# Odd layer: shares of the output projection as seven products of half depth; neighbourhood attention's bias tables by GpSimd

## The reference, cut to what matters

```
bias = rpb[:, d_row[:, None, None, :, None], d_col[None, :, :, None, :]]
s_loc = jnp.einsum('brnqhd,brnjwhd->bhrnqjw', qb, k_band.astype(f32)) + bias.astype(f32)[None]
s_loc = jnp.where(col_valid[:, :, None, :], s_loc, NEG_INF)
```

## Time and profile before

| | us |
|---|---|
| median of 3 runs | 3266.69 (3261.67 to 3269.23) |
| the profiled execution, its own time | 3264.15 |
| its span | 3262.4 |
| PE busy | 3063.6 (94%) |
| DVE busy | 1571.3 (48%) |
| ACT busy | 719.9 (22%) |
| POOL busy | 9.6 |

### The profile page before, as it was taken

The page is one execution under the profiler, slowest core; times in us unless marked ns, Lnnn a source line. Parts: engine busy times, 40 slices in busy tenths (PEclk is TensorE's granted clock), DMA queues, the critical chain, the costliest instruction groups (busy, mean ns, idle before and its releaser), DMA issues. The chain is left out here.

```text
span 3262.4 us, 40994 instructions
## 1 busy us (share of the span) xinstructions
PE 3063.6 (94%) x17092; PEld 1820.2 (56%) x17092; DVE 1571.3 (48%) x2473; ACT 719.9 (22%) x1217; POOL 9.6 (0%) x10
## 2 busy tenths in 40 slices
PE   7999999899998899999988998999999999999998
PEld 3475544447446733332322322587577887887875
DVE  4553248515957712212112121546486767566664
ACT  3110232403128110000000000000441333241413
POOL 0000000000000000000000000100000000000000
PEclk9999999999999899999999999999999999999999
DMA  7301144222111599999999999322112212121210
GB/s 280 129 3 53 54 163 153 74 80 100 44 48 73 207 386 428 427 428 428 427 428 428 427 428 419 141 99 97 57 52 78 78 53 78 62 92 54 78 52 27
DMA packets 122073, 588.20 MB, mean 180 GB/s; under 512 B 6944, under 2 KB 9248, under 8 KB 97696
## 3 DMA queue, kind: packets, MB, share of 16 engines
q1 hardware_dynamic: 121888, 585.57, 45.0%
HBM read 583.45 MB, written 2.10 MB: 179 GB/s over the span
## 5 line engine op out<-in xcount | busy, mean ns | idle before, releaser
L578 PE MATMUL ps<-hT,weight_ring 128*128 128x512 f32 (+1 forms) x1144 | 505.5, 599 | 4.9 <-PEq L491 3.4
L578 PEld LDWEIGHTS ps<-hT,weight_ring 128*128 128x128 f32 (+1 forms) x1144 | 216.2, 191 | 271.5 <-issue 269.2
L352 DVE TENSOR_TENSOR work<-work,ps 128x512 f32<-128x512 f32 x189 | 129.9, 687 | 207.0 <-PE ps L563 202.5
L563 PE MATMUL ps<-weight_ring 128*128 128x256 f32 x992 | 224.8, 379 | 0.0
L2687 PE MATMUL ps<-work 128*64 128x512 f32 x832 | 189.3, 597 | 25.5 <-DMA work<-in_w_up 16.4
L578 PE MATMUL ps<-work,weight_ring 128*128 128x512 f32 (+1 forms) x496 | 211.9, 574 | 0.3 <-PEq L491 0.3
L2852 DVE SCALAR_TENSOR_TENSOR xT<-ps,mod,xT 128x512 f32<-128x512 f32 x128 | 96.1, 751 | 229.8 <-PE ps L2701 220.0
L2687 PE MATMUL ps<-weight_ring,work 128*64 128x512 f32 x800 | 181.7, 597 | 21.0 <-DMA weight_ring<-in_w_up 13.2
L563 PEld LDWEIGHTS ps<-weight_ring 128*128 128x128 f32 x992 | 186.9, 190 | 24.8
L563 PE MATMUL ps<-weight_ring,spare_slot 128*128 128x256 f32 x800 | 181.6, 380 | 0.0
L563 PEld LDWEIGHTS ps<-weight_ring,spare_slot 128*128 128x128 f32 x800 | 151.0, 190 | 21.0 <-issue 0.7
(11 more groups left out here) (488 smaller groups left out, 4206.2 us busy)
## 6 DMA issues: line engine op xcount, KB each, us to landing
work<-in_w_up SPq DMA_DIRECT2D x27, 2048.0 KB, 42.5
weight_ring<-in_w_gate SPq DMA_DIRECT2D x26, 2048.0 KB, 45.2
work<-in_w_gate SPq DMA_DIRECT2D x25, 2048.0 KB, 45.2
weight_ring<-in_w_down SPq DMA_DIRECT2D x24, 2048.0 KB, 44.2
weight_ring<-in_w_up SPq DMA_DIRECT2D x24, 2048.0 KB, 42.4
work<-in_w_down SPq DMA_DIRECT2D x24, 2048.0 KB, 45.1
weight_ring<-in_w_in_odd SPq DMA_DIRECT2D x20, 2048.0 KB, 7.8
weight_ring<-in_w_in SPq DMA_DIRECT2D x16, 2048.0 KB, 11.1
```

What stands on the lines that cost most here:

```text
L352: v(dve.tensor_tensor(out, x, got, op), sig if out is steps[-1][0] else None)
L563: ins = pe.matmul(bank[:, j * L:(j + 1) * L], st, mv, start=k == 0, stop=k == 3)
L578: ins = pe.matmul(bank[0:m, 0:f], w[:, k, where:where + m], src[:, k, 0:ntok], start=k == 0, stop=k == kt - 1)
```

## The change

**Shares.** For G > 0 the share of the output projection is no longer 8 tiles, but 14: each half of the 1024 columns is done by seven products of half depth, 2 x 128 rows by 256 columns for each quarter (`kt // 2` matmuls in place of 4 for each half of a product). Four activation sums of 128 x 512 are put into B, the weight sums of the first half into I and of the second half behind tiles tS + 1 to tS + 4. The chain's links stand behind every second of the 14 tiles, the weight sums of block Q behind tS + 8 to tS + 11. New rooms hold the sums: `share_sums`, a part of the masks, a quarter of Z, and `mstage` for u.

**Tables.** GpSimd prepares them (`prepare_tables`), with two instructions for each head: heads 0 and 1 in the mixer's projection, heads 2 to 7 beside the attention, each as soon as it is loaded. VectorE only waits on `tables_ready`.

```diff
-ODD_SUMMED = [0, 1, 2, 3, 4] + [6 * G - 1 + i for G in range(1, 4) for i in (0, 1, 2, 4, 5)]
+ODD_SUMMED = [(i, 0) for i in range(5)] + [(6 * G - 1 + i, half) for G in range(1, 4)
+                                           for i, half in ((0, 0), (1, 0), (2, 0), (3, 0), (3, 1), (4, 0), (5, 0))]
...
+        n, c = w.shape[1] // 2, 512 * half
+        j = self.sum_order[i, half]
+        rooms = [room[:, 0:n, :] for room in self.w_rooms]
...
-                        for k in range(4):
+                        for k in range(kt // 2):
...
+def prepare_tables(ch, heads):
+
+    loaded, ready = ch.S["bias_loaded"], ch.S["tables_ready"]
+
+    def part(pool):
+        p = Line(pool, ch.S["pool_step"])
+        for h in heads:
+            p.after(loaded, 16 * (h + 1))
+            t = bias_table(ch, h).rearrange("p (r c) -> p r c", c=64)
+            p(pool.tensor_scalar(t, t, HD ** 0.5, None, MUL))
+            p(pool.tensor_tensor(t, t, ch.m("win")[:, 0:64].unsqueeze(1).to_broadcast([P, 14, 64]), ADD), ready)
+    return part
...
         def prepare(line, dve, j=j):
-            for h in (2 * j, 2 * j + 1):
-                line.after(loaded, 16 * (h + 1))
-                t = tab[h % 4].rearrange("p (r c) -> p r c", c=64)
-                line(dve.scalar_tensor_tensor(t, t, HD ** 0.5, ch.m("win")[:, 0:64].unsqueeze(1).to_broadcast([P, 14, 64]),
-                                              MUL, ADD))
+            line.after(ready, 2 * j + 2)
...
+    share_rooms = [ch.share_sums[:, :], ch.msk[:, dead:dead + 2 * L], None, ch.msk[:, dead + 2 * L:dead + 4 * L]]
+    share_copy = ch.mstage[:, :, :].rearrange("p a c -> p (a c)")
+    rooms = [x.rearrange("p (k t) -> p k t", t=L) if n != 2 else Z[:, 0:2, L:T] for n, x in enumerate(share_rooms)]
+    share = (Z[:, 0:2, 0:L], Z[:, 0:2, L:T], Z[:, 2:4, 0:L], Z[:, 2:4, L:T]), tuple(rooms)
+
+    ns, b0 = (14, 1) if G else (0, 0)
...
-        tiles += [(3,) + t[1:] for t in share_tiles(ch, Z, 8, 1)]
+        seven_into_stream(ch, tiles, 3, 0, share, share_copy)
+        seven_into_stream(ch, tiles, 3, 4, share, share_copy, half=1, before=lambda a: a.after(by_dve, 24))
...
-    chain = [tS + 1 + i for i in range(7)] if G else [tQ + 1 + i for i in range(7)]
+    chain = [tS + 1 + 2 * i for i in range(7)] if G else [tQ + 1 + i for i in range(7)]
...
-        beside.add((tS if G else tI) + 1 + n, vector=weight_sum(ch, first + b0 + 3, n))
+        beside.add((tS + 7 if G else tI) + 1 + n, vector=weight_sum(ch, first + b0 + 3, n))
+        if G:
+            beside.add(tB + 2 + n, vector=activation_sum(ch, n, share))
+            beside.add(tI + 1 + n, vector=weight_sum(ch, first + 3, n))
+            beside.add(tS + 1 + n, vector=weight_sum(ch, first + 3, n, 1))
```

More of the change, by code:

```diff
@@ L94 @@
 HALF_MASKS = ["L16", "L", "U16", "Uoff", "I", "quarter"]
+NMASK = len(MASKS) * P + len(HALF_MASKS) * 64
 def mask_arrays():
@@ L138, in __init__ @@
         self.eps = sb("eps", [P, 4])
+        self.share_sums = sb("share_sums", [P, 2 * L])
         self.ps = ctx.enter_context(nc.psum_tensor("ps", [P, BANKS, 512], F32))
@@ L157, in __init__ @@
         own = len(block1_plan(arrays)) - 2
-        summed = [own, own + 1, out, out + 1] + [last + i for i in EVEN_SUMMED] + [last + 15 + i for i in ODD_SUMMED]
+        summed = [own, own + 1, out, out + 1] + [last + i for i in EVEN_SUMMED]
+        summed = [(i, 0) for i in summed] + [(last + 15 + i, half) for i, half in ODD_SUMMED]
         self.sum_order = {i: j for j, i in enumerate(summed)}
@@ L284, in nothing, with weight_sum @@
     pass
-def weight_sum(ch, i, n):
+def weight_sum(ch, i, n, half=0):
     def part(v, dve):
-        (a11, a12, a21, a22), (s1, s2, s3, s4) = ch.weight_parts(i)
+        (a11, a12, a21, a22), (s1, s2, s3, s4) = ch.weight_parts(i, half)
         if n == 0:
@@ L360, in seven_tiles, with seven_into_stream @@
         tiles.append((b, ("W", p, natural), 0, None, T, evictions[p]))
-def seven_into_stream(ch, tiles, b, n, source, room, gains=None):
+def seven_into_stream(ch, tiles, b, n, source, room, gains=None, half=0, before=None):
     d11, d12, d21, d22 = quarters(ch.xT[:, n:n + 4, :])
@@ L376, in first @@
     def first(a, act, ps, sig):
+        if before:
+            before(a)
         a(act.copy(u, taken(ps)), sig)
@@ L403, in seven_into_stream @@
     for p in STREAM_ORDER:
-        tiles.append((b, ("W", p, False), 0, source, T, evictions[p]))
+        tiles.append((b, ("W", p, False, half), 0, source, T, evictions[p]))
 STREAM_ORDER = (1, 2, 6, 7, 5, 4, 3)
@@ L435, in quarters, with product_operands @@
     return x[:, 0:2, 0:L], x[:, 0:2, L:T], x[:, 2:4, 0:L], x[:, 2:4, L:T]
-def product_operands(ch, i, p, source):
-    (a11, a12, a21, a22), (s1, s2, s3, s4) = ch.weight_parts(i)
+def product_operands(ch, i, p, source, half):
+    (a11, a12, a21, a22), (s1, s2, s3, s4) = ch.weight_parts(i, half)
     (b11, b12, b21, b22), (t1, t2, t3, t4) = ch.activation_parts(source)
@@ L547, in _ @@
                 if kind[0] == "W":
-                    a_, b_, need_w, need_h = product_operands(ch, i, kind[1], src)
+                    half = kind[3] if len(kind) > 3 else 0
+                    a_, b_, need_w, need_h = product_operands(ch, i, kind[1], src, half)
                     if need_w:
-                        pe.wait_ge(weight_ready.sem, 4 * ch.sum_order[i] + need_w)
+                        pe.wait_ge(weight_ready.sem, 4 * ch.sum_order[i, half] + need_w)
                     if (norm or src is not None) and need_h:
@@ L562, in _ @@
                             st, mv = (b_[:, k, cols], a_[:, k, :]) if kind[2] else (a_[:, k, cols], b_[:, k, :])
-                            ins = pe.matmul(bank[:, j * L:(j + 1) * L], st, mv, start=k == 0, stop=k == 3)
+                            ins = pe.matmul(bank[:, j * L:(j + 1) * L], st, mv, start=k == 0, stop=k == kt // 2 - 1)
                 elif kind == "M":
@@ L586, in _ @@
                 tensor_beside.get(n, nothing)(pe)
+        if extra_pool:
+            @block.gpsimd
+            def _(pool):
+                extra_pool(pool)
         @block.scalar
@@ L980, in _ @@
         ch.stream(sp, 6)
-        load(ch.msk[:, 2 * P:], A["masks"][:, 2 * P:], got_rest)
+        load(ch.msk[:, 2 * P:NMASK], A["masks"][:, 2 * P:], got_rest)
     def modulation(pe, n):
@@ L2269, in conv_norm, with bias_table @@
     return (total, square_total), (square, take_root, finish), (centre, scale)
+def bias_table(ch, h):
+    flat = ch.slot((10, 9)[h % 4 // 2]).rearrange("p a t -> p (a t)")
+    return flat[:, h % 2 * 896:(h % 2 + 1) * 896]
+def prepare_tables(ch, heads):
[8 more added lines that the diff above has]
+    return part
 def neighbourhood_attention(ch, block, finish_convolution):
@@ L2277, in neighbourhood_attention @@
     v = v[:, 0:6, :]
-    flat = [ch.slot(i).rearrange("p a t -> p (a t)") for i in (10, 9)]
-    tab = [flat[i // 2][:, (i % 2) * 896:(i % 2 + 1) * 896] for i in range(4)]
-    loaded = ch.S["bias_loaded"]
+    tab = [bias_table(ch, i) for i in range(4)]
+    loaded, ready = ch.S["bias_loaded"], ch.S["tables_ready"]
     def load(sp):
@@ L2340, in neighbourhood_attention @@
             beside.add(-1, scalar=finish_convolution)
-    beside.project(ch, 0, [], extra_sync=load)
+    beside.project(ch, 0, [], extra_sync=load, extra_pool=prepare_tables(ch, range(2, 8)))
 def block2_mixer(ch, norm):
@@ L2352, in block2_mixer @@
     loaded = ch.counter("bias_loaded")
+    ch.counter("tables_ready")
     def load_tables(sp):
```

19 lines of the change are left out of this document (10 added, 9 removed).

## The result

The changed kernel takes 3299.80 us (median of 4, 3298.66 to 3300.96), the kernel before 3264.75 (median of 4, 3261.67 to 3269.23). The ratio is 1.0104, 95% interval 1.0092 to 1.0116: slower by 35 us, where 3292 and +27 were forecast. The sign, and the engine that makes it, are as forecast; the sum was some 8 us short.

The account below looks back on a forecast made before the run. TensorE was taken to bound stage S and VectorE the attention, with VectorE binding S after the change. 3264.15 + 28.5 (queue) + 8 (clock) - 10 (tables) = 3290.7, given as 3292 us, range 3272 to 3308.

Parts of the forecast that it names:

- What bounds S: Stage S, groups 1 to 3: VectorE becomes the bound with 42.6 us of work, against 33.7 on TensorE.
- the rival in which TensorE goes on binding: Stage S: it shrinks by 4.0 us a group and the tables give 10, total 3242; chance 6%.
- 44 us or more: Sign in S of group 1: VectorE's busy time there, which was 29.0 us before.
- the 4.0 us of the sum: TensorE in S: 14 half-depth products cost 24.2 us where eight tiles cost 28.2.
- The late start: VectorE reaches S late from sums in B and I; TensorE waits 4.2 us ahead of turn(1).
- The rival without a late start: Sums in B and I fall into pauses; Q begins 1 us later, total 3257 or 3265; chance 9%.
- The queue's price, 28.5: VectorE's queue through S: Q begins 9.5 us later in each group, +28.5 us for three groups.
- The clock's price, 8: Low clock behind two pauses a group in S, 1.7 us of work each: 0 to 10 us, taken as +8.
- The tables, -10: Attention: tables leave VectorE; 8.3 us of waits and 2.7 of low clock go, 1 us lost to GpSimd meetings.
- a meeting costs 0.2 us: Attention: VectorE scalings meeting GpSimd instructions, about 11 in all, 2.4 us at most, taken as +1.
- The rival that GpSimd blocks VectorE: Attention: scalings wait for GpSimd's end; tables gain nothing or cost 2, total 3301 to 3304; chance 12%.
- The sum: Whole kernel: 3264.15 + 28.5 + 8 - 10 = 3290.7, given as 3292; the forecast holds 68%.

Follow-up runs that it names:

- e6: Shares alone (tables on VectorE) with block Q's four weight sums in S cut to one column in groups 1 to 3: 3294.63 us, +30.0 against before.
- e11: The changed kernel with matrix products of no use put into TensorE's three long pauses of S: 3289.89 us, +22.2 against before.
- e4: Shares alone (tables on VectorE) with the activation sums in B and weight sums in I cut to one column: 3294.27 us, +29.7 against before.
- e10: The changed kernel, both parts, measured a third time: 3300.58 us, +32.8 against the kernel before.

## Why the prediction was right, and where it was short

**What bounds S.** Right. VectorE was busy for 42.4 us in the window of S, the sum was 42.6; TensorE waits for L3515, and the rival in which TensorE goes on binding is out by this and by e6. That the two figures agree to 0.2 us is partly luck: the window also holds 6.4 us of VectorE's work for stage I, and the last seven instructions of S's own come after it. Of the signs that the prediction named, "44 us or more" was thus missed, and S is 49.9 us long where 47 to 49 were named. TensorE's own work in S fell by less than the 4.0 us of the sum. Without its waits (4.01, 0.85, 0.42, 2.42, 1.11 and 3.49) S at full clock is 35.4 us, 2.7 under the old 38.13. It costs nothing here, because TensorE waits.

**The late start.** Right. The walk gave pauses of 4.2, 0.8, 0.8, 2.7, 1.6 and 3.7 us. Measured in the changed kernel: 4.01, none, 0.42, 2.42, 1.11 and 3.49. The one at link 0 is hidden behind products at the low clock; in e11, at full clock, it is there with 0.85. The rival without a late start is out, since e4, which takes only the lateness away, gains about 8 us.

**The queue's price, 28.5.** Nearly right. At full clock S is longer by 9.6 us (47.70 against 38.13), where 9.5 was taken. Another 0.5 a group lies ahead of S, of it 0.26 in a wait at the last product of block I. Three groups: 10.1 x 3 = 30.3.

**The clock's price, 8.** The step that was mis-sized. Its upper bound of 10 assumed two pauses a group with 1.7 us of lost work each, the length from the earlier trace rows. Around turn(1) the stretch was twice as long, 6.8 us. It cost 3.6 x 3 = 10.8 us by the groups' distance, and e11 is 10.7 under e10. The row that the length came from is itself one of two cases: behind the same pause of 4.00 us, at the same place, the changed kernel has 6.8 us at 1.2 GHz, and the 32 instructions take 9.79 us instead of 9.01.

**The tables, -10.** Right in what they remove: 3.78 became 1.52. It was -7.9. The step that failed is "a meeting costs 0.2 us": it rested on the one row in which both engines run, and GpSimd's instruction there has one input. The rival that GpSimd blocks VectorE was right in its mechanism for the additions, and wrong in its size: it let every meeting block to the end, while only three scalings in the changed kernel were held by more than 0.4 us, for 1.0, 1.7 and 1.9 us over their 0.62. The tables therefore still gain. No table came late.

**The sum.** 30.3 + 10.8 - 7.9 = 33.2, where 28.5 + 8 - 10 = 26.5 was forecast and 35, 38 and 33 were measured. Of the 6.7 us between the sums 1.8 are the queue, 2.8 the clock and 2.1 the tables: three terms off in the same direction, each by a little. Part by part the sum fits less well, 41.1 against the 37.6 and 39.0 of the shares alone and 7.9 against the 11.0 and 10.8 of the tables alone, some 3 us each; the 3 us by which the profiled execution of the kernel before lies under the medians are of that size. 3299.8 lies within 3272 to 3308.

## What to carry to other kernels

Before work is taken from the engine that binds and paid with another's, count what the other has to do between two points at which the first waits for it, and walk through its queue row by row: the busy share of the whole kernel (49% for VectorE) says nothing about it, and the walk gave the lengthening of S at full clock to 0.1 us (9.5 against 9.57). Add what the clock takes behind each new pause, by its own rows, and leave room above it: one row shows one case, and here the same pause had stretches of two lengths behind it. And measure the two halves of such a change apart: here the one with the tables was worth keeping alone (3256 us, 0.3% under the kernel before), and the sum hid it.

## What the runs showed of the hardware

- A scaling of VectorE (128x768, 0.62 us alone) that begins beside a GpSimd tensor_tensor lasts until 0.4 us after that has ended, up to 2.49 us in the changed kernel and 2.56 in e10. One that began 0.06 us ahead of it (978.74 in the changed kernel, GpSimd at 978.80) took its 0.62 and GpSimd's instruction 2.52 instead of 2.08. Beside a GpSimd tensor_scalar a scaling takes 0.62 to 1.26: one that began 0.6 us into it ended 1.1 us before its end, one that began 1.4 us into it wasn't held, and one that began 1.6 us into it lasted until 0.4 us after its end.
- The Trainium skill (SBUF — State Buffer, "Who interferes with whom") says that where a VectorE instruction in a mode with two ports meets one of GpSimd, the second to issue "fully blocks". Whether the scaling is in such a mode no run here shows. The trace agrees for the GpSimd instruction with two inputs; beside that with one the hold is shorter than the instruction.
- On GpSimd the instruction with two inputs was the quicker one: 2.08 us for 128x896 with a broadcast second operand, 2.45 with one input. The prediction had bounded the first by 2.7 and 5.4.
- In the changed kernel a pause of TensorE of 4.01 us came with 6.8 us at 1.2 GHz in each group, the pause of 3.49 with 3.4 us. The length of the pause alone doesn't settle this: in e6 the pause of 4.00 us came with 3.4 us in groups 2 and 3, and in e4 that of 3.30 at link 6 with 6.8 in groups 2 and 3. The pause of 2.42 us at link 3 had 3.4 us behind it in all three groups of e4 and none in the changed kernel. A pause of 2.05 us elsewhere was followed by a low stretch in some kernels and not in others (8.83 or 7.14 us for the same 32 instructions).
- Matrix products of no use in the pauses keep TensorE at 2.4 GHz behind them: turn(1) 1.97 us instead of 3.67, and 10.7 us of the kernel's time (e11 against e10).
